# Reading a pair's first bank ahead of the next unit's low part, and adding its sums a unit later

## The chip, the cores and the metric

The kernel runs on one core of a Trainium2 chip. The metric is the time of one execution on the device in microseconds (us), as the median of several runs. TensorE (PE in the rows) multiplies; VectorE (DVE) and ScalarE (ACT) split operands, empty PSUM banks and do the elementwise work; GpSimd (POOL) and SyncE (SP, which issues the loads) help. The engines run on their own and meet at semaphores.

## The reference

Two transformer blocks run one after the other on x, 256 tokens by 2048 channels in float32. The attention, convolution and recurrence parts are not touched by this change. What is touched is where the two MLPs add their last product to x:

```python
def first_block(x, ...):
    ...
        x = x + merged @ w_out[l]
        h = rms_norm(x, norm_mlp_g[l]) @ w_mlp_up[l]             # 2048 -> 8192
        x = x + jnp.square(jax.nn.relu(h)) @ w_mlp_down[l]       # 8192 -> 2048

def second_block(x, ...):
    ...
        x = x + mix @ w_out[l]
        h2 = _rms_norm(x, norm2_g[l])
        x = x + (jax.nn.silu(h2 @ w_gate[l]) * (h2 @ w_up[l])) @ w_down[l]   # 2048 -> 5632 -> 2048
```

## The kernel before

**A product in two parts.** Every float32 operand is split into a high part, rounded to the type that TensorE multiplies fast, and a low part, the rest. A product is high by high, plus low by high, plus high by low. A weight tile of 1 MB (128 rows by 4 blocks of 512) is a *unit*. SyncE loads it into `raw` (four buffers), ScalarE writes its high part `whi` (line 422), VectorE subtracts and writes its low part `wlo` (line 430, `lo_unit`), and TensorE runs first the products with `whi`, then those with `wlo`. `whi` and `wlo` have two buffers each, so ScalarE and VectorE work at most about one unit ahead of TensorE. Semaphores `hi_split`, `lo_split` and `units_used` count these steps.

**A pair.** In the last product of the first MLP (kind `scaled`: six pairs in `PAIRS1`, since the result is multiplied by the squared inverse norm) and in the whole second MLP (17 pairs in `PAIRS`, kinds `gate` and `down`) two blocks of 512 output columns are made at once, for two halves of 128 tokens. The four results stand in four PSUM banks `acc[:, b, m]`, here called bank (b, m). A scaled pair has 8 units, as have a gate pair and the later down pairs; the first two down pairs have 6. In an ordinary unit TensorE runs 24 matmuls, 6 for each bank. In the first and the last unit of a pair it does so bank by bank (`plain_products`): in the first, it waits in `bank_free` before each bank until VectorE has read what the pair before left there; in the last, it raises `bank_done` after each bank, and `units_used` after bank (1, 1).

**Seven units.** Two units of a pair (numbers 3 and 5; in the second MLP's first two down pairs number 3 alone, then 1 and 3) use seven products of sums in the place of eight: 21 matmuls (`seven_products`, `seven_low`). Part of their results lands in other banks, `sd` and `tp`. After the pair's last `lo_unit` VectorE runs `combine`: three instructions that make `vw` and `yz` from `tp`, `sd` and `q_sum` (ScalarE's copy of `sd`, counted by `q_copied`) and raise the semaphore `combined` three times.

**How a pair ends.** VectorE has then seven or eight instructions to do on x (`xres`): four that add the banks (`bank_to_x`, lines 2350 and 2352) and three or four that add `q_sum`, `vw` and `yz` (`sums_to_x`, lines 2364 and 2371 to 2375). For a scaled pair `finish_scaled` holds all of them, in the order bank (0, 0), bank (0, 1), sums, bank (1, 0), bank (1, 1); for a down pair `finish_first` and `finish` give the same order. All of it stands behind the `lo_unit` of the next unit. That next unit is the first of another pair, or, after the second scaled pair of each of three quarters, the first unit of the MLP's up product (`up_products`, line 474), which needs both banks (0, m). A gate pair is not added to x: its first bank is read by `finish_first` *ahead* of the next `lo_unit`, and the others behind it.

**What sets the order.** Each engine's program is written out by hand, one function per engine with plain Python loops; the order of the calls is the order of the instructions. Nothing is scheduled. A boundary between pairs, in what follows, is the last unit of one pair and the first of what comes after. Three boundaries lead from a scaled pair to a scaled pair, three from a scaled pair to an up product, and five out of a down pair (three to the other down pair, two to a gate pair). The last down pair has no successor.

Of the kernel before, what the change touches and what calls it, by code (L numbers as in the profile page):

```python
# [35 lines left out]
MT = T // P  # L36
# [89 lines left out]
def build(nc, t, out):  # L126

    ctx = ExitStack()
    with ctx:
# [409 lines left out]
        PAIRS = []  # L539
# [12 lines left out]
        for p in PAIRS1 + PAIRS:  # L552
            ahead = PAIRS1[:p.n] if p.kind == "scaled" else PAIRS1 + PAIRS[:p.n]
            p.order = len(ahead)
            p.combined = sum(3 if q.kind == "gate" else 6 for q in ahead)
            p.gates = sum(q.kind == "gate" for q in ahead)
            p.sevens = sum(len(q.seven) for q in ahead)
            p.seven_units = [q.unit + v for q in ahead for v in q.seven]
            p.q_sum = q_sums[p.kind != "scaled"]
# [911 lines left out]
        def _(pe):  # L1471
# [271 lines left out]
            def seven_products(p, v, hi, lo):  # L1743
# [11 lines left out]
                if first:  # L1755

                    if p.order:
                        pe.wait_ge(combined, p.combined)
                        pe.wait_ge(q_copied, p.order)
                    if p.kind == "scaled":  # L1760
                        pe.wait_ge(read_dve, read_first(PAIRS1[p.n // 2 * 2]))
                    else:
                        pe.wait_ge(op_lo, T_HID2 + p.turned * MT)
# [159 lines left out]
        def _(dve):  # L1923
# [453 lines left out]

            def finish_scaled(p):

                for m in range(MT):  # L2380
                    bank_to_x(p, 0, m)
                dve.wait_ge(read_dve, read_first(p) + MT)
                sums_to_x(p)
                for m in range(MT):
                    bank_to_x(p, 1, m)

# [30 lines left out]
            for i in range(QUARTERS):  # L2417
                for p in PAIRS1[2 * i:2 * i + 2]:
                    for v in range(p.units):
                        if v in p.seven:  # L2420
                            seven_low(p, v)
                        else:
                            lo_unit(dve, (p.unit + v) // UN, v % UN)
                        if p.chunk[1] == 0 and v == 0:
                            hidden_squares(i * UN + UN - 1, i * 2 * UN + G_DLOOP)
                        if p.chunk[1] == 0 and v == 1:
                            hidden_lo(i * UN + UN - 1, UN - 1)
                        if p.chunk[1] and v == 0:
                            finish_scaled(PAIRS1[p.n - 1])
                        if v == p.units - 1:  # L2430
                            combine(p)
                for c in range(UN):
                    g = i * 2 * UN + G_DLOOP + UN + c
                    for j in range(UN):
                        lo_unit(dve, g, j)
                        if c == 0 and j == 0:
                            finish_scaled(PAIRS1[2 * i + 1])
                        if c and j == 0:
# [166 lines left out]
            def finish(p):  # L2605

                if p.kind == "down":
                    bank_to_x(p, 0, 1)
                    if p is not PAIRS[-1]:
                        dve.wait_ge(bank_read, 4 * p.n + MT)  # L2610
                        sums_to_x(p)
                    for m in range(MT):
# [13 lines left out]
            for p in PAIRS:  # L2626
                for v in range(p.units):
                    if v == 0 and p.n and PAIRS[p.n - 1].kind == "gate":
                        finish_first(PAIRS[p.n - 1])
                    if v in p.seven:  # L2630
                        seven_low(p, v)
                    else:
                        lo_unit(dve, (p.unit + v) // UN, (p.unit + v) % UN)
                    if v == 0 and p.n and PAIRS[p.n - 1].kind == "down":
                        finish_first(PAIRS[p.n - 1])
                    if p.n == 0 and v < UN:
# [35 lines left out]
```

## Time and profile before

| | |
|---|---|
| median of 3 runs | 2473.7 us (2473.68 to 2473.72) |
| the profiled execution: time | 2474.51 us |
| the profiled execution: span of the core | 2472.8 us |
| TensorE busy | 2453.8 us, 99% |
| VectorE busy | 1708.5 us, 69% |
| ScalarE busy | 1212.2 us, 49% |
| chain that ended last | PE 93%, DVE 4%, ACT 1%, issue 1% |
| mean DMA rate | 189 GB/s |

The rows are of one profiled execution. In a timeline each row has the start and the duration in us; `x2` says that two such instructions followed each other, and a bracket says how long the engine had been idle before and what it waited for. `L2350` is line 2350 of the kernel before. A row of a matmul lasts longer than the distance to the next, because matmuls overlap; it is the distance between starts that adds up to time.

### The profile page before, as it was taken

Reading aid. Unit: us, or ns where it says so; the run is one execution under the profiler, and the core shown is the slowest. Engines: PE = TensorE matmul, PEld = TensorE weight load, DVE = VectorE, ACT = ScalarE, POOL = GpSimd, SP = SyncE. Lnnn points to the kernel's source line nnn. Section 1 sums busy time; section 2 is a strip of 40 time slices with the busy share of each in tenths; the row PEclk is TensorE's granted clock in tenths of the full one; section 3 lists DMA queues with packets and bytes.
Section 4 is the critical chain, followed back from the end, with each engine's and each line's share of the span. In section 5 each row is a group of like instructions: output and inputs, shape, how many; then the busy total and the mean of one; then the engine's idle time right before and its main releaser. Section 6 shows DMA issues by size and latency. Waiting matters only on the chain.

```text
span 2472.8 us, 28758 instructions
## 1 busy us (share of the span) xinstructions
PE 2453.8 (99%) x11719; PEld 2047.9 (83%) x11719; DVE 1708.5 (69%) x1590; ACT 1212.2 (49%) x1270; POOL 116.6 (5%) x95
## 2 busy tenths in 40 slices
PE   9999999999999999999999999999999999999999
PEld 8888888888888878888888888788888788878887
DVE  5775455454655785776765558886788878887887
ACT  5545534343344444544444448875555444544553
POOL 0410010010110000000000010000200000000000
PEclk9999999999999999999999999999999999999999
DMA  7555465666655565655665655444556565655654
GB/s 252 173 184 180 160 192 192 196 194 196 230 184 187 187 201 188 197 192 175 201 194 192 209 171 189 153 151 162 180 191 199 190 194 185 207 195 191 203 187 153
DMA packets 233138, 467.18 MB, mean 189 GB/s; under 512 B 13424, under 2 KB 25216, under 8 KB 232622
## 3 DMA queue, kind: packets, MB, share of 16 engines
q1 hardware_dynamic: 231454, 460.09, 57.4%
q10 hardware_dynamic: 1552, 5.25, 0.6%
q8 instruction: 93, 1.52, 0.3%
q14 instruction: 39, 0.32, 0.0%
HBM read 463.20 MB, written 2.10 MB: 188 GB/s over the span
## 4 chain that ended last, share of the span: by engine, by line
PE 93%; DVE 4%; ACT 1%; issue 1%; POOL 0%; DMA 0%; ACTq 0%; DVEq 0%; POOLq 0%
PE acc L445 13%; PE acc L454 13%; PE acc L447 13%; PE acc L1714 9%; PE acc L1715 9%; PE acc L1718 9%; PE acc L474 5%; PE acc L480 2%; PE sd L474 2%; PE tp L474 2%; DVE wlo L430 1%; PE tp L480 1%; PE sd L480 1%; PE acc L1772 1%; PE acc L1768 1%; PE acc L1769 1%
## 5 line engine op out<-in xcount | busy, mean ns | idle before, releaser
L430 DVE TENSOR_TENSOR wlo<-raw,whi 128x2048 fp32r<-128x2048 f32 (+1 forms) x396 | 913.5, 2308 | 642.9 <-ACT whi L422 641.8
L422 ACT ACTIVATE whi<-raw 128x2048 fp32r<-128x2048 f32 (+1 forms) x396 | 748.0, 1890 | 844.4 <-PE acc L454 356.4
L445 PE MATMUL acc<-whi,opA_hi 128*128 128x512 f32 x1152 | 454.8, 395 | 0.0
L447 PE MATMUL acc<-whi,opA_lo 128*128 128x512 f32 x1152 | 449.4, 390 | 0.0
L454 PE MATMUL acc<-wlo,opA_hi 128*128 128x512 f32 x1152 | 287.4, 391 | 0.2 <-DVE wlo L430 0.2
L445 PEld LDWEIGHTS acc<-whi,opA_hi 128*128 128x128 f32 x1152 | 216.9, 188 | 45.4 <-issue 0.9
L447 PEld LDWEIGHTS acc<-whi,opA_lo 128*128 128x128 f32 x1152 | 216.8, 188 | 44.2
L454 PEld LDWEIGHTS acc<-wlo,opA_hi 128*128 128x128 f32 x1152 | 214.9, 188 | 44.8 <-DVE wlo L430 0.8
L1714 PE MATMUL acc<-whi,opA_hi 128*128 128x512 f32 x552 | 216.0, 391 | 5.9 <-DVE xres L2350 3.8
L1715 PE MATMUL acc<-whi,opA_lo 128*128 128x512 f32 x552 | 215.0, 389 | 0.0
L1714 PE MATMUL acc<-whi,opB 128*128 128x512 f32 x536 | 209.7, 391 | 1.4 <-DVE xres L2352 1.4
L1715 PE MATMUL acc<-whi,opB 128*128 128x512 f32 x536 | 208.7, 389 | 0.0
L474 PE MATMUL acc<-opB,whi 128*128 128x512 f32 x512 | 159.2, 392 | 1.1 <-DVE xres L2350 1.1
L445 PE MATMUL acc<-whi,opB 128*128 128x512 f32 (+1 forms) x384 | 147.5, 387 | 2.0 <-ACT whi L422 2.0
L1718 PE MATMUL acc<-wlo,opA_hi 128*128 128x512 f32 x552 | 148.1, 389 | 0.0
L447 PE MATMUL acc<-whi,opB 128*128 128x512 f32 (+1 forms) x384 | 145.1, 381 | 0.0
L1718 PE MATMUL acc<-wlo,opB 128*128 128x512 f32 x536 | 143.1, 389 | 0.0
L1714 PEld LDWEIGHTS acc<-whi,opA_hi 128*128 128x128 f32 x552 | 103.6, 188 | 30.4 <-DVE xres L2350 5.0
L1718 PEld LDWEIGHTS acc<-wlo,opA_hi 128*128 128x128 f32 x552 | 103.6, 188 | 21.7
L1715 PEld LDWEIGHTS acc<-whi,opA_lo 128*128 128x128 f32 x552 | 103.7, 188 | 21.0
L1714 PEld LDWEIGHTS acc<-whi,opB 128*128 128x128 f32 x536 | 100.6, 188 | 23.1 <-DVE xres L2352 2.2
L1718 PEld LDWEIGHTS acc<-wlo,opB 128*128 128x128 f32 x536 | 100.6, 188 | 20.9
(417 smaller groups left out, 3373.9 us busy)
## 6 DMA issues: line engine op xcount, KB each, us to landing
raw<-in_w_in SPq DMA_DIRECT2D x114, 1024.0 KB, 5.4
raw<-in_w_mlp_up SPq DMA_DIRECT2D x64, 1024.0 KB, 5.5
raw<-in_w_mlp_down SPq DMA_DIRECT2D x64, 1024.0 KB, 5.0
raw<-in_w_gate SPq DMA_DIRECT2D x88, 512.0 KB, 3.8
raw<-in_w_up SPq DMA_DIRECT2D x88, 512.0 KB, 4.7
raw<-in_w_down SPq DMA_DIRECT2D x88, 512.0 KB, 4.7
raw<-in_w_out SPq DMA_DIRECT2D x32, 1024.0 KB, 5.0
raw<-in_w_branch SPq DMA_DIRECT2D x16, 1024.0 KB, 5.0
```

Source lines behind the costliest of these rows:

```text
L422: eng.activation(whi[:, j % SPL, k, 0:cols], raw[:, j, k, 0:cols], ACT.Copy).then_inc(hi_split, share(k))
L430: eng.tensor_tensor(wlo[:, j % SPL, k, 0:cols], raw[:, j, k, 0:cols], whi[:, j % SPL, k, 0:cols].bitcast(F32), ALU.subtract).then_inc(lo_s ...
L445: eng.matmul(acc[:, pair, m, 0:cols], hi[:, kt + i, m * P:(m + 1) * P], whi[:, s, i, 0:cols], start=first and i == 0, stop=False)
L447: eng.matmul(acc[:, pair, m, 0:cols], lo[:, kt + i, m * P:(m + 1) * P], whi[:, s, i, 0:cols], start=False, stop=False)
L454: mm = eng.matmul(acc[:, pair, m, 0:cols], hi[:, kt + i, m * P:(m + 1) * P], wlo[:, s, i, 0:cols], start=False, stop=last and i == UK - 1)
L474: eng.matmul(up_bank(group, c), whi[:, s, i, c * P:(c + 1) * P], opB[:, UK * j + i, :, :].rearrange("p v t -> p (v t)"), start=j == 0 and ...
L480: mm = eng.matmul(up_bank(group, c)[:, 0:T], wlo[:, s, i, c * P:(c + 1) * P], opB[:, UK * j + i, 0, :], start=False, stop=j == UN - 1 and ...
L1714: pe.matmul(acc[:, b, m, :], hi[:, 2 * v + a, rows], whi[:, s, 2 * a + b, :], start=first and a == 0, stop=False)
L1715: pe.matmul(acc[:, b, m, :], lo[:, 2 * v + a, rows], whi[:, s, 2 * a + b, :], start=False, stop=False)
L1718: return pe.matmul(acc[:, b, m, :], hi[:, 2 * v + a, m * P:(m + 1) * P], wlo[:, s, 2 * a + b, :], start=False, stop=last and a == 1)
L1768: pe.matmul(bank, a_h, seven_hi[:, i, :], start=alone and first, stop=False)
L1769: pe.matmul(bank, a_l, seven_hi[:, i, :], start=False, stop=False)
```

## The change

The banks and the sums of a scaled or down pair are no longer added in one go behind the next `lo_unit`.

- Ahead of the `lo_unit` of the next pair's first unit VectorE now reads bank (0, 0); ahead of that of an up product, banks (0, 0) and (0, 1). The other banks follow behind that `lo_unit`.
- `sums_to_x` comes a unit later, behind the `lo_unit` (or `seven_low`) of the next unit, with a wait that the bank reads are done.
- TensorE's wait before a pair's first seven unit asks for the three steps of `combine` of the pair before (`p.sums_read`) and no longer for all six.

The numbers of instructions, their shapes and the programs of the other engines are the same but for that wait. The diff:

```diff
--- before.py
+++ after.py
@@ -553,6 +553,8 @@
             ahead = PAIRS1[:p.n] if p.kind == "scaled" else PAIRS1 + PAIRS[:p.n]
             p.order = len(ahead)
             p.combined = sum(3 if q.kind == "gate" else 6 for q in ahead)
+
+            p.sums_read = ahead[-1].combined + 3 if ahead else 0
             p.gates = sum(q.kind == "gate" for q in ahead)
             p.sevens = sum(len(q.seven) for q in ahead)
             p.seven_units = [q.unit + v for q in ahead for v in q.seven]
@@ -1755,7 +1757,7 @@
                 if first:
 
                     if p.order:
-                        pe.wait_ge(combined, p.combined)
+                        pe.wait_ge(combined, p.sums_read)
                         pe.wait_ge(q_copied, p.order)
                     if p.kind == "scaled":
                         pe.wait_ge(read_dve, read_first(PAIRS1[p.n // 2 * 2]))
@@ -2375,14 +2377,11 @@
                 dve.tensor_tensor(xres[:, :, n2], xres[:, :, n2], yz[:, :, :], ALU.add).then_inc(combined, 1)
                 dve.wait_ge(combined, p.combined + 6)
 
-            def finish_scaled(p):
-
-                for m in range(MT):
-                    bank_to_x(p, 0, m)
-                dve.wait_ge(read_dve, read_first(p) + MT)
-                sums_to_x(p)
-                for m in range(MT):
-                    bank_to_x(p, 1, m)
+            def banks_to_x(p, ahead):
+
+                for b, m in ((0, 0), (0, 1), (1, 0), (1, 1)):
+                    if ahead(b, m):
+                        bank_to_x(p, b, m)
 
             for n in range(UN):
                 for j in range(UN):
@@ -2417,6 +2416,8 @@
             for i in range(QUARTERS):
                 for p in PAIRS1[2 * i:2 * i + 2]:
                     for v in range(p.units):
+                        if p.chunk[1] and v == 0:
+                            banks_to_x(PAIRS1[p.n - 1], lambda b, m: (b, m) == (0, 0))
                         if v in p.seven:
                             seven_low(p, v)
                         else:
@@ -2426,15 +2427,23 @@
                         if p.chunk[1] == 0 and v == 1:
                             hidden_lo(i * UN + UN - 1, UN - 1)
                         if p.chunk[1] and v == 0:
-                            finish_scaled(PAIRS1[p.n - 1])
+                            banks_to_x(PAIRS1[p.n - 1], lambda b, m: (b, m) != (0, 0))
+                        if p.chunk[1] and v == 1:
+                            dve.wait_ge(read_dve, read_first(p))
+                            sums_to_x(PAIRS1[p.n - 1])
                         if v == p.units - 1:
                             combine(p)
                 for c in range(UN):
                     g = i * 2 * UN + G_DLOOP + UN + c
                     for j in range(UN):
+                        if c == 0 and j == 0:
+                            banks_to_x(PAIRS1[2 * i + 1], lambda b, m: b == 0)
                         lo_unit(dve, g, j)
                         if c == 0 and j == 0:
-                            finish_scaled(PAIRS1[2 * i + 1])
+                            banks_to_x(PAIRS1[2 * i + 1], lambda b, m: b == 1)
+                        if c == 0 and j == 1:
+                            dve.wait_ge(read_dve, read_first(PAIRS1[2 * i + 1]) + 2 * MT)
+                            sums_to_x(PAIRS1[2 * i + 1])
                         if c and j == 0:
                             hidden_squares((i + 1) * UN + c - 1, g)
                         if c and j == 1:
@@ -2606,9 +2615,6 @@
 
                 if p.kind == "down":
                     bank_to_x(p, 0, 1)
-                    if p is not PAIRS[-1]:
-                        dve.wait_ge(bank_read, 4 * p.n + MT)
-                        sums_to_x(p)
                     for m in range(MT):
                         bank_to_x(p, 1, m)
                     return
@@ -2625,14 +2631,15 @@
 
             for p in PAIRS:
                 for v in range(p.units):
-                    if v == 0 and p.n and PAIRS[p.n - 1].kind == "gate":
+                    if v == 0 and p.n:
                         finish_first(PAIRS[p.n - 1])
                     if v in p.seven:
                         seven_low(p, v)
                     else:
                         lo_unit(dve, (p.unit + v) // UN, (p.unit + v) % UN)
-                    if v == 0 and p.n and PAIRS[p.n - 1].kind == "down":
-                        finish_first(PAIRS[p.n - 1])
+                    if v == 1 and p.n and PAIRS[p.n - 1].kind == "down":
+                        dve.wait_ge(bank_read, 4 * p.n)
+                        sums_to_x(PAIRS[p.n - 1])
                     if p.n == 0 and v < UN:
                         side2(12 * UN + v)
                     if v == 0 and p.n:
```

The order of VectorE's instructions at three places follows. In the rows, `wlo<-raw,whi` is a `lo_unit`, `xres<-acc` a bank read, `xres<-` with `q_sum`, `vw` or `yz` a sum, and `t_sum` and `seven_lo` belong to `seven_low`. Lines 2338, 2350 and 2364 of before are lines 2340, 2352 and 2366 after.

VectorE, from `combine` of the first scaled pair of a quarter to the second pair's second unit, before:

```order
L2338 TENSOR_TENSOR yz<-vw,sd 128x1024
L430 TENSOR_TENSOR wlo<-raw,whi 128x2048
L2350 SCALAR_TENSOR_TENSOR xres<-acc,smalls,xres 128x512 x2
L2364 SCALAR_TENSOR_TENSOR xres<-q_sum,smalls,xres 128x512
L2364 SCALAR_TENSOR_TENSOR xres<-vw,rstd_neg,xres 128x512
L2364 SCALAR_TENSOR_TENSOR xres<-yz,smalls,xres 128x512 x2
L2350 SCALAR_TENSOR_TENSOR xres<-acc,smalls,xres 128x512 x2
L430 TENSOR_TENSOR wlo<-raw,whi 128x2048 x2
```

The same place of VectorE in the changed kernel:

```order
L2340 TENSOR_TENSOR yz<-vw,sd 128x1024
L2352 SCALAR_TENSOR_TENSOR xres<-acc,smalls,xres 128x512
L430 TENSOR_TENSOR wlo<-raw,whi 128x2048
L2352 SCALAR_TENSOR_TENSOR xres<-acc,smalls,xres 128x512 x3
L430 TENSOR_TENSOR wlo<-raw,whi 128x2048
L2366 SCALAR_TENSOR_TENSOR xres<-q_sum,smalls,xres 128x512
L2366 SCALAR_TENSOR_TENSOR xres<-vw,rstd_neg,xres 128x512
L2366 SCALAR_TENSOR_TENSOR xres<-yz,smalls,xres 128x512 x2
L430 TENSOR_TENSOR wlo<-raw,whi 128x2048
```

One bank read moved ahead of the low part, and the four sums moved behind the next low part. The boundaries out of a down pair, but for the one below, read the same with the lines of the down kind.

VectorE, from `combine` of a quarter's second scaled pair into the up product, in the changed kernel (before, it read as the first fence):

```order
L2340 TENSOR_TENSOR yz<-vw,sd 128x1024
L2352 SCALAR_TENSOR_TENSOR xres<-acc,smalls,xres 128x512 x2
L430 TENSOR_TENSOR wlo<-raw,whi 128x2048
L2352 SCALAR_TENSOR_TENSOR xres<-acc,smalls,xres 128x512 x2
L430 TENSOR_TENSOR wlo<-raw,whi 128x2048
L2366 SCALAR_TENSOR_TENSOR xres<-q_sum,smalls,xres 128x512
```

Here two bank reads stand ahead of the low part.

VectorE, from the first down pair of the second MLP into the second, whose unit 1 is a seven unit, before:

```order
L430 TENSOR_TENSOR wlo<-raw,whi 128x2048
L2352 TENSOR_TENSOR xres<-acc,xres 128x512 x2
L2371 TENSOR_TENSOR xres<-xres,q_sum_149 128x512
L2373 TENSOR_TENSOR xres<-xres,vw 128x512
L2375 TENSOR_TENSOR xres<-xres,yz 128x2x512
L2352 TENSOR_TENSOR xres<-acc,xres 128x512 x2
L2272 TENSOR_TENSOR t_sum<-raw 128x1024
```

The same place in the changed kernel:

```order
L430 TENSOR_TENSOR wlo<-raw,whi 128x2048
L2354 TENSOR_TENSOR xres<-acc,xres 128x512 x3
L2274 TENSOR_TENSOR t_sum<-raw 128x1024
L2277 TENSOR_TENSOR t_sum<-t_sum,raw 128x512
L2279 TENSOR_TENSOR t_sum<-t_sum,raw 128x512
L2283 TENSOR_TENSOR seven_lo<-raw,seven_hi 128x512
L2284 TENSOR_TENSOR seven_lo<-raw,seven_hi 128x1024
L2288 TENSOR_TENSOR seven_lo<-t_sum,seven_hi 128x2048
L2373 TENSOR_TENSOR xres<-xres,q_sum_149 128x512
L2375 TENSOR_TENSOR xres<-xres,vw 128x512
L2377 TENSOR_TENSOR xres<-xres,yz 128x2x512
L430 TENSOR_TENSOR wlo<-raw,whi 128x2048
```

Here the sums stand between unit 1, a seven unit, and the low part of unit 2.

## Rows read from the trace of the kernel before

**Rows 1.** The page: span, TensorE's busy time and share, and its granted clock.

```profile
span 2472.8 us, 28758 instructions
...
PE 2453.8 (99%) x11719; PEld 2047.9 (83%) x11719; DVE 1708.5 (69%) x1590; ACT 1212.2 (49%) x1270; POOL 116.6 (5%) x95
...
PEclk9999999999999999999999999999999999999999
```

**Rows 2.** TensorE's waits: total us, times, longest us.

```profile
PE acc L1714 <- DVE xres L2350: 3.8, 3, 1.3
PE acc L1714 <- DVE xres L2352: 3.5, 5, 0.7
...
PE acc L474 <- DVE xres L2350: 1.1, 3, 0.4
...
PE sd L1772 <- DVE seven_lo L2282: 0.5, 1, 0.5
```

**Rows 3.** Timeline of TensorE, first unit after a scaled pair: start, duration.

```profile
878.13 0.44 PE L1714 MATMUL acc<-whi,opA_hi 128*128 128x512 f32 x1
...
882.35 0.50 PE L1714 MATMUL acc<-whi,opA_hi 128*128 128x512 f32 x1 [1.27 <-DVE xres L2350]
...
885.20 0.39 PE L1714 MATMUL acc<-whi,opA_hi 128*128 128x512 f32 x1
```

**Rows 4.** Timeline of VectorE at the same boundary.

```profile
873.20 1.22 DVE L2338 TENSOR_TENSOR yz<-vw,sd 128x1024 f32<-128x1024 f32 x1
874.99 2.29 DVE L430 TENSOR_TENSOR wlo<-raw,whi 128x2048 fp32r<-128x2048 f32 x1 [0.57 <-ACT whi L422]
877.20 1.40 DVE L2350 SCALAR_TENSOR_TENSOR xres<-acc,smalls,xres 128x512 f32<-128x512 f32 x2
...
881.54 1.41 DVE L2350 SCALAR_TENSOR_TENSOR xres<-acc,smalls,xres 128x512 f32<-128x512 f32 x2
...
887.78 2.29 DVE L430 TENSOR_TENSOR wlo<-raw,whi 128x2048 fp32r<-128x2048 f32 x1 [2.63 <-ACT whi L422]
```

**Rows 5.** Timelines at a boundary from gate pair to gate pair: VectorE, TensorE.

```profile
1991.03 0.69 DVE L2603 TENSOR_TENSOR acc<-acc,q_sum 128x512 f32<-128x512 f32 x1
...
1994.82 0.39 PE L1714 MATMUL acc<-whi,opB 128*128 128x512 f32 x1
...
2000.27 1.03 PE L500 MATMUL tp<-ident,stage 128*128 128x128 f32 x8
```

**Rows 6.** Timeline of TensorE, last scaled matmuls and first up units.

```profile
921.47 0.61 PE L1718 MATMUL acc<-wlo,opA_hi 128*128 128x512 f32 x2
922.45 0.73 PE L474 MATMUL acc<-opB,whi 128*128 128x512 f32 x2 [0.37 <-DVE xres L2350]
...
928.13 0.63 PE L474 MATMUL acc<-opB,whi 128*128 128x512 f32 x2
...
933.70 0.63 PE L474 MATMUL acc<-opB,whi 128*128 128x512 f32 x2
```

**Rows 7.** Timeline of TensorE, first unit after the second down pair.

```profile
1951.61 0.39 PE L1714 MATMUL acc<-whi,opB 128*128 128x512 f32 x1
...
1958.10 0.39 PE L1714 MATMUL acc<-whi,opB 128*128 128x512 f32 x1
```

**Rows 8.** Timeline of TensorE, second down pair: starts of units 0 and 2.

```profile
1918.47 0.40 PE L1714 MATMUL acc<-whi,opA_hi 128*128 128x512 f32 x1
...
1930.53 0.39 PE L1714 MATMUL acc<-whi,opA_hi 128*128 128x512 f32 x1
```

**Rows 9.** Timeline of VectorE over the same units.

```profile
1918.86 0.69 DVE L2371 TENSOR_TENSOR xres<-xres,q_sum 128x512 f32<-128x512 f32 x1
...
1921.32 1.29 DVE L2352 TENSOR_TENSOR xres<-acc,xres 128x512 f32<-128x512 f32 x2
1922.53 1.22 DVE L2272 TENSOR_TENSOR t_sum<-raw 128x1024 f32<-128x1024 f32 x1
...
1926.85 2.29 DVE L2286 TENSOR_TENSOR seven_lo<-t_sum,seven_hi 128x2048 fp32r<-128x2048 f32 x1
```

## The prediction

> **What bounds the kernel now.** First the page's totals: TensorE is busy for 2453.8 of 2472.8 us, 99%, at the full granted clock in every slice [rows 1]. Only its idle time, some 19 us, and what stands around it can be won without taking products away. So the second view is TensorE's waits. Four of them are at ends of pairs: 3.8 us in 3 waits for a scaled bank read (line 2350), 3.5 us in 5 for a down bank read (line 2352), 1.1 us in 3 ahead of the up product, and 0.5 us once for the low part of a seven unit [rows 2]. Together 8.9 us. The third view is the timelines of TensorE and VectorE at one such place.
>
> At the first one, TensorE starts the new pair's bank (0, 0) at 878.13, has to start bank (1, 0) at 882.35 after 1.27 us of idleness, and comes to the second unit at 885.20 [rows 3]. VectorE meanwhile ends `combine` at 873.20 + 1.22 = 874.42, waits 0.57 us for ScalarE's high part, makes the low part from 874.99, reads two banks from 877.20, does the four sums, and reads the other two banks from 881.54 [rows 4]. The bank that TensorE waits for is late by the sums. They take 881.54 - 877.20 less two reads (1.40) = 2.9 us.
>
> **What a stall costs.** I take distances between starts and not the bracketed idleness. A clean first unit is the one after a gate pair: 2000.27 - 1994.82 = 5.45 us for 24 matmuls, 0.227 us each [rows 5]. Against it:
> - Scaled to scaled: 885.20 - 878.13 = 7.07 [rows 3], excess 1.62. Three times, by the waits view of nearly one size (3.8 us, longest 1.3) [rows 2]: 4.9 us.
> - Scaled to up: the last two scaled matmuls start at 921.47, so the up product could start at 921.47 + 2 x 0.227 = 921.92. It starts at 922.45, and its first unit takes 928.13 - 922.45 = 5.68, where the next takes 933.70 - 928.13 = 5.57 [rows 6]. Excess 0.53 + 0.11 = 0.64, three times: 1.9 us.
> - Out of a down pair: 1958.10 - 1951.61 = 6.49 [rows 7], excess 1.04. Four of the five: 4.2 us.
> - The fifth, into the pair whose unit 1 is a seven unit: units 0 and 1 take 1930.53 - 1918.47 = 12.06 [rows 8], clean 5.45 + 21 x 0.227 = 10.22. Excess 1.8 us, both waits of that pair in it.
>
> Sum: 4.9 + 1.9 + 4.2 + 1.8 = 12.8 us.
>
> The excess of 1.62 is more than the 1.27 us in the bracket, since the first matmuls after a wait are also further apart than 0.227. By the brackets alone the sum would be 8.9 us. The Trainium skill ("Perfetto Trace Analysis", section "Tensor Engine Instruction (MATMUL, LD_WEIGHTS)") says that the reported end of a matmul is estimated from its size and not observed. By that page idleness, which is counted from such an end, is not to be summed, and distances of starts are, which gives the 12.8; the trace agrees, as the rows above differ by those 0.35 us.
>
> **The change, part by part.**
>
> *Bank (0, 0) ahead of the low part.* It costs one read, 0.7 us (half of 1.40 [rows 4]), in front of an instruction that TensorE needs. The read can begin when `combine` is done, at 874.42, and its bank is done too: TensorE's last unit starts at 878.13 - 5.45 = 872.68 and is through with bank (0, 0) after a quarter, at 874.04, plus the tail of a matmul and the signal, together some 0.3 us. VectorE then stood idle for 0.57 us until 874.99 [rows 4], so the read ends at about 875.1 and the low part starts 0.1 to 0.2 us later than before. It ends at 877.4. TensorE needs it behind the first four matmuls of the new pair, at 878.13 + 0.91 = 879.04. Margin 1.6 us: the read costs nothing. The nearest row that shows such a read is the one after a gate pair: VectorE does it ahead of the low part at 1991.03, and that unit is the clean one [rows 5]. There it stands at eleven boundaries. From this row I take the cost as zero; the upper bound is 0.2 us at each of eleven places, 2.2 us, if nothing hid it.
>
> *The other banks right behind.* (0, 1) is read by 878.0, (1, 0) by 878.7, and (1, 1), whose products end only with the unit at 878.13, by about 879.4. TensorE needs them at 879.5, 880.9 and 882.2, a quarter of a unit apart. Margins 1.5, 2.2 and 2.8 us, so no stall remains at the plain boundaries. A down bank read is a plain add and no longer than that.
>
> *Two banks ahead of the up product.* Bank (0, 1) is done half a unit into TensorE's last unit, at 921.92 - 2.72 = 919.2 plus 0.3. Its read ends at 920.2, and TensorE wants it at 921.92. The low part then runs to about 922.5; TensorE wants it behind 16 matmuls, at 925.55. It comes 1.4 us later than before, and with it the release of its `raw` buffer and a load that SyncE has queued behind that. That buffer's next user is four units away, so I charge nothing.
>
> *The sums a unit later.* The same 2.9 us now stand behind the low part of unit 1. Ahead of unit 2's low part VectorE was idle for 2.63 us, waiting for ScalarE [rows 4], and the sums and a read have left unit 0, which brings unit 1's low part forward by up to 2.5 us (it then waits for its own high part). So low part 2 can start as soon as its high part is there; it is needed 3.6 us into unit 2, and the margin is over 4 us. What waits for the sums, `q_copied` and `combine` of the new pair, is four units away. The loads don't wait for them.
>
> *The tightest place.* In the second down pair unit 1 is a seven unit. Its `t_sum` starts at 1922.53 less the sums (1921.32 - 1918.86 = 2.46) less one read (0.6) = 1919.5 [rows 9]. The last `seven_lo` starts 1926.85 - 1922.53 = 4.32 later, at 1923.8, when the part that TensorE waited 0.5 us for is just done; TensorE wants that at 1918.47 + 5.45 + 1.36 = 1925.3. That wait goes too. Then come 2.3 us, the sums (2.46) and unit 2's low part (2.2), to 1930.7, and unit 3, again a seven unit, has its first low parts at 1930.7 + 4.3 = 1935.0. TensorE, now ahead by 1.8 us, wants them at 1918.47 + 5.45 + 4.77 + 5.45 + 1.36 = 1935.5. Margin 0.5 us; if it fails, a few tenths, once.
>
> *The wait on* `combined`. At unit 1 of that pair TensorE would otherwise wait for sums that stand behind the low parts it needs. With the weaker wait it asks for `combine`, done a unit before. Cost zero.
>
> So the sum stays 12.8 us, with bounds 12.8 and 12.8 - 2.2 - 0.3 = 10.3; it cannot be above the excess measured, since nothing else on TensorE is taken away. The profiled execution takes 2474.5 us, 0.8 above the median: it should come to 2461.7, its span to 2460.0, and the median to 2473.7 - 12.8 = **2460.9 us**. The last down pair and its stores are unchanged.
>
> **The rivals.**
>
> *Only the bracketed idleness comes back.* If the wider spacing after a wait belonged to the start of a pair, 8.9 us would go: 2464.8. Against it: a gate boundary has no such spacing [rows 5]. 10%.
>
> *The first bank is reported late (the other side).* VectorE runs in order, and now waits at `bank_done` ahead of the low part. If that signal came only with the last unit's end, the read would run from 878.3 to 879.0 and the low part to 881.3, 2.3 us after TensorE wants it: 8 x 2.3. The up products would get their two banks about 1.6 us after the unit's end: 3 x 1.6. That is 23.2 us new against 12.8 gone: 2473.7 + 10.4 = 2484.1. It begins to cost from a delay of 1.6 us, the low part's margin, and makes the kernel slower from about 2.8 us. Against it: the read after a gate pair at 1991.03, which waits for the same signal, starts 1.7 us and not a whole unit into TensorE's last unit (which began at 1994.82 - 5.45 = 1989.37) [rows 5]. 5%, and another 3% for a part of it that leaves the time where it was. The Trainium skill (same page, same section) lets a matmul push its semaphore update once PSUM has acknowledged its bytes; by that the delay is a tail of the single matmul, and this rival is void; the row at 1991.03 agrees.
>
> *The change doesn't free TensorE.* If its waits before banks (0, 1) and (1, 0) counted reads in another order than VectorE now makes them, the stalls would stay: 2473.7. Both go (0, 0), (0, 1), (1, 0), (1, 1), so 4%.
>
> **How the numbers follow.** Forecast 2460.9 with 78%, its own bounds 2460 to 2463.4. Only the idleness: 10%. Late signal: 5% slower, 3% no change; no effect: 4%. The range reaches from 2459.5, for stalls that were a little larger than the rows, to 2465.0, which takes in the second case. A measurement of this kernel can tell about 0.2%, 4.9 us, from no change. Faster by more: 0.78 + 0.10 = 0.88; within: 0.07; slower: 0.05.
>
> **What would show it.** In TensorE's waits the rows for lines 2350 and 2352 (now 2352 and 2354) and for `seven_lo` are gone; the first unit of every pair takes 5.45 us, and the up product starts 0.227 us after the last scaled matmul. VectorE's read of bank (0, 0) starts right behind `combine`, at the latest 2 us into TensorE's last unit. Wrong it would be if TensorE waited for `wlo` (line 430) in a first unit, if units 2 or 3 of a pair took longer, or if the spans of the boundaries shrank and others grew.

## The result, and the profile after

| | before | after |
|---|---|---|
| median | 2473.68 us | 2460.62 us |
| the profiled execution: time | 2474.51 us | 2460.66 us |
| its span | 2472.8 us | 2458.9 us |
| TensorE busy | 2453.8 us | 2448.9 us |
| chain that ended last, PE share | 93% | 97% |

The changed kernel is faster by 13.1 us, ratio 0.9947 with a 95% interval of 0.9932 to 0.9962. The forecast was 2460.9 us. The medians are of five executions each; one of the five of the changed kernel took 5014.87 us, twice the others, for a reason that nothing on record shows, and the ratio leaves it out.

The page of the changed kernel, its totals, the granted clock and the shares of the chain that ended last (answers to [rows 1]):

```profile
span 2458.9 us, 28747 instructions
...
PE 2448.9 (100%) x11719; PEld 2048.8 (83%) x11719; DVE 1707.2 (69%) x1590; ACT 1212.4 (49%) x1270; POOL 116.6 (5%) x95
...
PEclk9999999999999999999999999999999999999999
...
PE 97%; DVE 1%; ACT 1%; issue 0%; POOL 0%; DMA 0%; ACTq 0%; DVEq 0%; POOLq 0%
```

TensorE's waits in the changed kernel, all of them (total us, times, longest us):

```profile
PE acc L445 <- ACT whi L422: 2.0, 3, 1.1
PE sd L1633 <- POOL ones L832: 1.2, 1, 1.2
PE tp L1825 <- ACT q2T L1305: 0.8, 1, 0.8
PE sd L1650 <- DMA gain_rows<-in_norm_mix_g: 0.7, 1, 0.7
PE tp L500 <- POOL stage L911: 0.7, 1, 0.7
PE tp L500 <- DVE opA_lo L512: 0.4, 1, 0.4
PE acc L454 <- DVE wlo L430: 0.2, 1, 0.2
```

All four rows of [rows 2] are gone: no wait for a bank read, none ahead of the up product, none for the low part of the seven unit. The others were there before and are elsewhere in the kernel. The 11 instructions that the page has fewer are semaphore instructions of VectorE (741, not 752); the computing instructions are the same in number.

The first boundary between scaled pairs, timeline of VectorE in the changed kernel:

```profile
872.21 1.22 DVE L2340 TENSOR_TENSOR yz<-vw,sd 128x1024 f32<-128x1024 f32 x1
873.35 0.74 DVE L2352 SCALAR_TENSOR_TENSOR xres<-acc,smalls,xres 128x512 f32<-128x512 f32 x1
874.01 2.28 DVE L430 TENSOR_TENSOR wlo<-raw,whi 128x2048 fp32r<-128x2048 f32 x1
876.21 2.06 DVE L2352 SCALAR_TENSOR_TENSOR xres<-acc,smalls,xres 128x512 f32<-128x512 f32 x3
879.44 2.29 DVE L430 TENSOR_TENSOR wlo<-raw,whi 128x2048 fp32r<-128x2048 f32 x1 [1.17 <-ACT whi L422]
...
885.18 2.29 DVE L430 TENSOR_TENSOR wlo<-raw,whi 128x2048 fp32r<-128x2048 f32 x1 [0.68 <-ACT whi L422]
```

TensorE at the same place: the last unit, the new pair's first and second unit.

```profile
871.69 0.39 PE L1716 MATMUL acc<-whi,opA_hi 128*128 128x512 f32 x1
...
877.13 0.39 PE L1716 MATMUL acc<-whi,opA_hi 128*128 128x512 f32 x1
...
882.57 0.39 PE L1716 MATMUL acc<-whi,opA_hi 128*128 128x512 f32 x1
```

The first unit takes 882.57 - 877.13 = 5.44 us where [rows 3] showed 7.07. VectorE reads the first bank in what was its 0.57 us of idleness in [rows 4]; the low part follows without a gap, 2.32 us after the start of TensorE's last unit as before (2.31), and the sums, between the two later low parts, still leave 0.68 us ahead of unit 2.

Before the up product the changed TensorE shows this, last scaled matmuls and first two up units:

```profile
918.84 0.61 PE L1720 MATMUL acc<-wlo,opA_hi 128*128 128x512 f32 x2
919.29 0.62 PE L474 MATMUL acc<-opB,whi 128*128 128x512 f32 x2
...
924.83 0.63 PE L474 MATMUL acc<-opB,whi 128*128 128x512 f32 x2
```

The step is 0.45 us, two matmuls; in [rows 6] it was 0.98. VectorE there reads the second bank and then makes the low part:

```profile
916.78 0.75 DVE L2352 SCALAR_TENSOR_TENSOR xres<-acc,smalls,xres 128x512 f32<-128x512 f32 x1 [0.53 <-PE acc L1720]
917.44 2.28 DVE L430 TENSOR_TENSOR wlo<-raw,whi 128x2048 fp32r<-128x2048 f32 x1
```

**What the profile has besides.** The span fell by 13.9 us, the median by 13.1. The first place that the change touches lies at 870 us, and TensorE was already 1.0 us ahead there. The difference is in the first microseconds. The first row of eight low-part matmuls (line 454) after 40 us of the span starts at 41.60 before and at 40.63 after; over all runs below this mark lies between 40.24 and 43.48. So spans compare only from this mark on. Before, 2472.8 - 41.60 = 2431.2; after, 2458.9 - 40.63 = 2418.3, which is 12.9 us less. TensorE's busy time fell too, by 4.9 us, though it runs the same 11719 matmuls: the wider spacing, after a wait and in the first microseconds, counts as busy in the page, and the brackets miss it.

### The profile page after: what moved, and what is told of

Read it like the earlier page. It is cut to its first block, busy times and chain, and to the rows that moved or that the text cites. A ratio compares the mean times of both kernels' runs of the same rounds, so it can differ in the third digit from the quotient of the medians.

```text
span 2458.9 us, 28747 instructions
## 1 busy us (share of the span) xinstructions
PE 2448.9 (100%) x11719; PEld 2048.8 (83%) x11719; DVE 1707.2 (69%) x1590; ACT 1212.4 (49%) x1270; POOL 116.6 (5%) x95
## 4 chain that ended last, share of the span: by engine, by line
PE 97%; DVE 1%; ACT 1%; issue 0%; POOL 0%; DMA 0%; ACTq 0%; DVEq 0%; POOLq 0%
PE acc L454 13%; PE acc L445 13%; PE acc L447 13%; PE acc L1716 10%; PE acc L1717 10%; PE acc L1720 10%; PE acc L474 5%; PE acc L480 2%; PE tp L474 2%; PE sd L474 2%; PE sd L480 1%; PE tp L480 1%; PE acc L1774 1%; PE acc L1771 1%; PE acc L1770 1%; PE tp L500 1%
```

## The experiments

All were built from the changed kernel unless said otherwise. "From the mark" is the span less the start of that row, which takes the start-up out; it is of one profiled execution of each run, and the two of the changed kernel (the one above and e5) agree within 0.1 us. e5 is the changed kernel once more, on one chip with e6 to e8.

> The changed kernel itself, beside the next three on one chip. 2460.6 us, 13.1 us under the kernel before; the mark for the three others.

It took 2460.90 us, ratio 0.9947 (0.9932 to 0.9962).

| run | median us | span | mark | from the mark | against e5 |
|---|---|---|---|---|---|
| before (the profiled execution) | 2473.8 (beside e5) | 2472.8 | 41.60 | 2431.2 | +12.8 |
| e1 scaled only | 2466.63 | 2465.3 | 41.03 | 2424.3 | +5.9 |
| e2 down only | 2467.88 | 2466.5 | 41.30 | 2425.2 | +6.8 |
| e3 sums later only | 2463.78 | 2462.5 | 41.48 | 2421.0 | +2.7 |
| e4 bank ahead only | 2466.74 | 2465.8 | 41.60 | 2424.2 | +5.8 |
| e5 the changed kernel | 2460.90 | 2458.6 | 40.24 | 2418.4 | 0 |
| e6 two banks ahead | 2461.16 | 2458.9 | 40.26 | 2418.6 | +0.3 |
| e7 three banks ahead | 2469.10 | 2468.4 | 41.72 | 2426.7 | +8.3 |
| e8 strong wait | 2467.87 | 2468.6 | 43.48 | 2425.1 | +6.8 |
| e9 thin sums, after | 2460.85 | 2458.2 | 40.44 | 2417.8 | -0.6 |
| e10 thin sums, before | 2462.84 | 2460.3 | 40.24 | 2420.1 | +1.7 |
| e11 up ahead, sums later | 2461.50 | 2460.2 | 41.23 | 2419.0 | +0.6 |

### Each half alone (e1, e2)

e1 puts the down pairs back, e2 the scaled pairs.

```diff
--- e1
                     bank_to_x(p, 0, 1)
+                    if p is not PAIRS[-1]:
+                        dve.wait_ge(bank_read, 4 * p.n + MT)
+                        sums_to_x(p)
...
-                    if v == 0 and p.n:
+                    if v == 0 and p.n and PAIRS[p.n - 1].kind == "gate":
                         finish_first(PAIRS[p.n - 1])
...
-                    if v == 1 and p.n and PAIRS[p.n - 1].kind == "down":
-                        dve.wait_ge(bank_read, 4 * p.n)
-                        sums_to_x(PAIRS[p.n - 1])
+                    if v == 0 and p.n and PAIRS[p.n - 1].kind == "down":
+                        finish_first(PAIRS[p.n - 1])
```

> Only the scaled pairs have the change; the second MLP's down pairs end as before. By my sum (distances between starts) 4.9 + 1.9 = 6.8 us go: 2473.7 - 6.8 = 2466.9 us. By the bracketed idleness alone 3.8 + 1.1 = 4.9 us go: 2468.8 us. In TensorE's waits the rows for the scaled bank reads are gone and the one for the down bank reads (3.5 us, 5 times) stays.

> Only the down pairs have the change; the scaled pairs end as before. By my sum 4.2 + 1.8 = 6.0 us go: 2467.7 us. By the bracketed idleness 3.5 + 0.5 = 4.0 us go: 2469.7 us. The waits for scaled bank reads stay (3.8 and 1.1 us), those for down bank reads and for the low part of the seven unit are gone. If the two halves are independent, their gains add up to that of the whole change, 13.1 us.

e1 took 2466.63 us, ratio 0.9971 (0.996 to 0.9982); e2 2467.88, ratio 0.9976 (0.9967 to 0.9985). From the mark e1 is 6.9 us under before and e2 6.0, together 12.9, the whole change; by the medians, against the kernel before beside them (2473.96), it is 7.3 and 6.1. My sums were 6.8 and 6.0, those of the brackets 4.9 and 4.0. Of the rows of [rows 2] each keeps the other half's, and only those. TensorE's waits of e1:

```profile
PE acc L1716 <- DVE xres L2354: 3.5, 5, 0.7
...
PE sd L1774 <- DVE seven_lo L2284: 0.5, 1, 0.5
```

So the halves are independent, and a stall costs what the starts say, not what its bracket says.

### Which of the two moves does it (e3, e4, e11)

e3 leaves all bank reads behind the low part and moves only the sums. e4 reads ahead and leaves the sums in place. e11 is e3 with the two banks ahead of the up product.

```diff
--- e3 (e11 has these hunks, but not the two of the up product)
-                        if p.chunk[1] and v == 0:
-                            banks_to_x(PAIRS1[p.n - 1], lambda b, m: (b, m) == (0, 0))
...
-                            banks_to_x(PAIRS1[p.n - 1], lambda b, m: (b, m) != (0, 0))
+                            banks_to_x(PAIRS1[p.n - 1], lambda b, m: True)
...
-                        if c == 0 and j == 0:
-                            banks_to_x(PAIRS1[2 * i + 1], lambda b, m: b == 0)
...
-                            banks_to_x(PAIRS1[2 * i + 1], lambda b, m: b == 1)
+                            banks_to_x(PAIRS1[2 * i + 1], lambda b, m: True)
--- e4
                         if p.chunk[1] and v == 0:
-                            banks_to_x(PAIRS1[p.n - 1], lambda b, m: (b, m) != (0, 0))
-                        if p.chunk[1] and v == 1:
-                            dve.wait_ge(read_dve, read_first(p))
+                            bank_to_x(PAIRS1[p.n - 1], 0, 1)
+                            dve.wait_ge(read_dve, read_first(PAIRS1[p.n - 1]) + MT)
                             sums_to_x(PAIRS1[p.n - 1])
+                            banks_to_x(PAIRS1[p.n - 1], lambda b, m: b == 1)
```

The down pairs and, in e4, the up product have the same.

> All four bank reads stand behind the next low part as before, and only the sums come a unit later. Theory: the sums were what made bank (1, 0) late, and bank (0, 0) was in time anyway (read at 877.95, wanted at 878.13), so almost everything at the eight plain boundaries goes; left are the up products' 3 x 0.64 = 1.9 us and some 0.07 us at each of eight boundaries: 2460.6 + 2.4 = 2463.0 us. Rival: the first bank's read ahead of the low part is what frees TensorE; then most of the 13 us stay and the time is near 2472.

> The first bank (both first banks before an up product) is read ahead of the low part, and the sums stay where they were, between banks (0, 1) and (1, 0). Theory: bank (1, 0) of a scaled pair is read at 8.85 us after the start of TensorE's last unit and wanted at 8.16, so 0.7 us of idleness (0.85 with the slower first matmuls) stays three times; of a down pair at 8.4, so 0.4 us stays four times, and about 1.3 us in the pair whose unit 1 is a seven unit; nothing before the up products. Left 2.6 + 1.6 + 1.3 = 5.5 us: 2460.6 + 5.5 = 2466.1 us. Rival (the read ahead does it all): 2460.6 us.

> The sums a unit later, and both first banks ahead of the low part before an up product, but at the eight plain boundaries no bank is read ahead. Theory: bank (0, 0) is read 0.1 to 0.2 us before TensorE wants it, and only the spacing of its first matmuls suffers, 0.06 to 0.1 us at each of eight boundaries: 0.5 to 0.8 us above the changed kernel, 2461.4 to 2461.7 us. If the read ahead at the plain boundaries is worth nothing at all: 2460.9 us.

e3: 2463.78 us, ratio 0.9958 (0.9942 to 0.9975). The sums a unit later are four fifths of the gain: 10.2 of 12.8 us from the mark. The expectation had 2.4 us left; from the mark it is 2.7, and the 0.3 us between them are lost in unit 3 of the second down pair (below, at e11). Most of what is left is the wait before the up product, unchanged, 0.7 us each time from start to start:

```profile
PE acc L474 <- DVE xres L2352: 1.1, 3, 0.4
```

e4: 2466.74 us, ratio 0.9972 (0.9962 to 0.9983), 5.8 us above the changed kernel where 5.5 were expected. TensorE's waits of e4, then its bank (1, 0) after a scaled pair, and the same after the second down pair:

```profile
PE acc L1716 <- DVE xres L2352: 2.0, 3, 0.7
...
PE sd L1774 <- DVE seven_lo L2284: 0.5, 1, 0.5
```

```profile
880.37 0.61 PE L1720 MATMUL acc<-wlo,opA_hi 128*128 128x512 f32 x2
881.66 0.50 PE L1716 MATMUL acc<-whi,opA_hi 128*128 128x512 f32 x1 [0.68 <-DVE xres L2352]
...
1949.32 0.61 PE L1720 MATMUL acc<-wlo,opB 128*128 128x512 f32 x2
1950.05 0.50 PE L1716 MATMUL acc<-whi,opB 128*128 128x512 f32 x1
```

After the scaled pair 0.68 us are in a bracket. After the down pair TensorE starts 0.73 us behind the two matmuls that take 0.45, so it waited 0.28 us, and no bracket and no row of the waits says so. The row of the two matmuls is 0.61 us long and ends at 1949.93, so that most of this short wait lies inside it.

e11: 2461.50 us, ratio 0.9949 (0.9933 to 0.9966), 0.6 us above the changed kernel both by the medians and from the mark, in the range expected. So the read ahead at the eight plain boundaries is worth 0.6 us in all. But it is not spread over the eight as the expectation had it. Set beside the changed kernel's, matmul by matmul, TensorE of e11 loses 0.1 us at each of the three scaled boundaries, at most 0.03 us at each down boundary, and 0.3 us at one place more: unit 3 of the second down pair, the tightest place of the prediction. There the read that stands behind the low part makes the whole chain of low parts later, and the first product with a low part starts 0.40 us after the one before it, not 0.227 (e3 loses the same 0.3 us):

```profile
1928.27 0.39 PE L1771 MATMUL acc<-seven_hi,ad_lo 128*128 128x512 f32 x1
1928.67 0.50 PE L1774 MATMUL sd<-seven_lo,opA_hi 128*128 128x512 f32 x1
```

The range was met, but half of the loss came from a place that the expectation did not name. At the first scaled boundary of e11 TensorE's first row of the new pair lasts 0.43 us, not 0.39:

```profile
877.76 0.43 PE L1716 MATMUL acc<-whi,opA_hi 128*128 128x512 f32 x1
```

That agrees with the bank being ready only just in time, as in [rows 3], where the same row lasts 0.44. Before the up product the read ahead is worth 2.1 us (e3 against e11), 0.7 for each of three.

### The length of the sums (e9, e10)

Both add only one column in 512 of `q_sum`, `vw` and `yz`; e9 from the changed kernel, e10 from the kernel before.

```diff
-                        ins = dve.scalar_tensor_tensor(xres[:, m, n], src, by[:, m:m + 1], xres[:, m, n], ALU.mult, ALU.add)
+                        c1 = slice(n.start, n.start + 1)
+                        ins = dve.scalar_tensor_tensor(xres[:, m, c1], src[:, 0:1], by[:, m:m + 1], xres[:, m, c1], ALU.mult, ALU.add)
...
```

The three additions of the down kind are cut to one column in the same way.

> The changed kernel, with its sums cut to one column of 512 (the rest of q_sum, vw and yz is never added to x, so the output isn't the reference's). VectorE saves some 2.3 us at each of eleven boundaries. Theory: where the change puts the sums they cost nothing, so nothing is won: 2460.9 us as the changed kernel on this chip, at most 0.3 us less from the last pair's end. Rival (the sums still delay low parts a unit later, in a way the waits don't show): over 1 us less.

> The kernel before, with its sums cut to one column in the same way (the output isn't the reference's). Everything stands in the old order. Theory: the length of the sums was the whole cause of the stalls at the eight plain boundaries, so bank (1, 0) is in time and they vanish; the three up products still wait for bank (0, 1), which is read ahead of the sums: 3 x 0.64 us. As with the sums a unit later: 2463.3 to 2463.8 us. Rival (the order of the first read matters there too): above 2466 us.

e9: 2460.85 us against 2460.90, and 0.6 us less from the mark. The traces say where the 0.6 us are: in the end of the last pair, whose sums and bank reads have no TensorE work behind them. TensorE's last matmuls of the changed kernel (first line) and of e9 (second):

```profile
2454.61 0.61 PE L1720 MATMUL acc<-wlo,opA_hi 128*128 128x512 f32 x2
...
2454.43 0.61 PE L1720 MATMUL acc<-wlo,opA_hi 128*128 128x512 f32 x2
```

From the mark to this row it is 2454.61 - 40.63 = 2413.98 us and 2454.43 - 40.44 = 2413.99; from the row to the end 4.3 and 3.8. So where the change puts them the sums cost TensorE nothing, and the thin ones save 0.5 us at the end, not the 0.3 at most that I had given. The medians, 0.05 us apart, don't show it, since the start-up scatters by more.

e10: 2462.84 us, ratio 0.9955 (0.994 to 0.997), half a microsecond below the range that I gave. That half is the same end: from e10's last matmuls, at 2456.49, it is 3.8 us too. Of the 11.1 us that it gains from the mark 10.6 are stalls that go with no instruction moved. Only the row before the up product stays in its waits (1.1 us, 3 times). Up to the last matmuls e10 is 0.5 us better than e3, and 0.3 of them are the tightest place, where e10 loses nothing. So two ways of taking the sums out from between the banks, later or shorter, agree within 0.5 us.

### How much margin the low part has (e6, e7)

```diff
--- e6 (e7 has 3 where this has 2)
-                            banks_to_x(PAIRS1[p.n - 1], lambda b, m: (b, m) == (0, 0))
+                            banks_to_x(PAIRS1[p.n - 1], lambda b, m: 2 * b + m < 2)
...
-                            banks_to_x(PAIRS1[p.n - 1], lambda b, m: (b, m) != (0, 0))
+                            banks_to_x(PAIRS1[p.n - 1], lambda b, m: 2 * b + m >= 2)
...
-                    bank_to_x(p, 0, 0)
+                    for k in range(2 if p is not PAIRS[-1] else 1):
+                        bank_to_x(p, k // 2, k % 2)
...
```

> At the plain boundaries banks (0, 0) and (0, 1) are read ahead of the low part, as before an up product. T is the start of TensorE's last unit. Bank (0, 1) is reported at T + 2.93 (in the changed kernel's trace the read before an up product starts 2.93 us after T), so the low part runs from T + 3.6 to T + 5.9 and is wanted at T + 5.44 + 0.91 = 6.35: margin 0.45 us. Theory: no cost at seven boundaries; at the eighth, whose unit 1 is a seven unit, the chain to unit 3 has a margin of 0.48 us and comes 0.8 us later, so 0.3 us are lost once: 2460.9 us. If a bank were reported only at the end of the unit, the low part would end at T + 9.1 or later and 2.8 us be lost at each of eight boundaries: 2483 us.

> Banks (0, 0), (0, 1) and (1, 0) are read ahead of the low part at the plain boundaries. Bank (1, 0) is reported at T + 4.29, the low part runs from T + 4.95 to T + 7.25 and is wanted at T + 6.35. Theory: TensorE waits 0.9 us for the low part, 1.1 us with the slower matmuls behind the wait, at each of eight boundaries, and 0.2 us more once: 2460.6 + 9.0 = 2469.6 us, still faster than before. In TensorE's waits a row for line 454's kind of low part in the pairs (wlo, line 430) appears eight times. Rival (the low part has more slack than I think): 2460.6 us.

e6: 2461.16 us, 0.3 above e5 as expected. The loss is where it was placed, and set beside the changed kernel's matmuls nowhere else. TensorE of e6 in unit 3 of the second down pair, last product with the high part and first with the low one:

```profile
1927.01 0.39 PE L1771 MATMUL acc<-seven_hi,ad_lo 128*128 128x512 f32 x1
1927.43 0.50 PE L1774 MATMUL sd<-seven_lo,opA_hi 128*128 128x512 f32 x1
```

The step is 0.42 and not 0.227. The changed kernel shows the 0.48 us of margin that e6 used up: there VectorE's part ends at 1925.89 + 1.22 = 1927.11 and TensorE takes it at 1927.59.

```profile
1925.89 1.22 DVE L2284 TENSOR_TENSOR seven_lo<-raw,seven_hi 128x1024 fp32r<-128x1024 f32 x1
...
1927.59 0.39 PE L1774 MATMUL sd<-seven_lo,opA_hi 128*128 128x512 f32 x1
```

e7: 2469.10 us, ratio 0.998 (0.9971 to 0.999), 8.2 us above e5 (9.0 expected). From start to start it loses 1.0 to 1.1 us at each of the eight boundaries; of the 0.2 us more that the expectation had for unit 3 only 0.05 is there. Its waits and VectorE at the first boundary:

```profile
PE acc L1720 <- DVE wlo L430: 5.9, 8, 0.8
```

```profile
874.47 0.74 DVE L2352 SCALAR_TENSOR_TENSOR xres<-acc,smalls,xres 128x512 f32<-128x512 f32 x1
875.74 0.75 DVE L2352 SCALAR_TENSOR_TENSOR xres<-acc,smalls,xres 128x512 f32<-128x512 f32 x1 [0.52 <-PE acc L1720]
877.10 0.75 DVE L2352 SCALAR_TENSOR_TENSOR xres<-acc,smalls,xres 128x512 f32<-128x512 f32 x1 [0.61 <-PE acc L1720]
877.77 2.28 DVE L430 TENSOR_TENSOR wlo<-raw,whi 128x2048 fp32r<-128x2048 f32 x1
```

The reads follow each other by the quarter of a unit that a bank takes, 877.10 - 875.74 = 1.36 us. Each bank is reported by itself, which settles the rival of a late signal, and TensorE's new wait is for the low part, eight times, 0.8 us at most. The order "banks first" is thus free for one, nearly free for two, and costs most of the gain for three.

### The wait on `combined` (e8)

```diff
-                        pe.wait_ge(combined, p.sums_read)
+                        pe.wait_ge(combined, p.combined)
```

> TensorE's wait ahead of a pair's first seven unit asks again for all six steps of the pair before, the sums too. Theory: at one place only, the pair whose first seven unit is unit 1, the sums stand behind that unit's low parts: they end at 1920.40 in the changed kernel's trace, and TensorE could start the unit at 1916.03. It loses 4.4 us once, 2465.0 us; elsewhere the first seven unit is unit 3 and the sums are long done. Rival (the weaker wait matters nowhere): 2460.6 us.

e8: 2467.87 us, ratio 0.9976 (0.9967 to 0.9986), 7.0 us above e5, where 4.4 were expected. The place is the expected one, and the only one. TensorE of e8 at unit 1 of the second down pair and at unit 2:

```profile
1918.41 0.61 PE L1720 MATMUL acc<-wlo,opA_hi 128*128 128x512 f32 x2
1923.29 0.79 PE L1770 MATMUL sd<-seven_hi,opA_hi 128*128 128x512 f32 x1 [4.27 <-DVE xres L2377]
1923.88 0.63 PE L1771 MATMUL sd<-seven_hi,opA_lo 128*128 128x512 f32 x1
1924.31 0.63 PE L1770 MATMUL acc<-seven_hi,opA_hi 128*128 128x512 f32 x1
...
1927.72 0.63 PE L1771 MATMUL sd<-seven_hi,ad_lo 128*128 128x512 f32 x1
1928.15 0.46 PE L1770 MATMUL tp<-seven_hi,ad_hi 128*128 128x512 f32 x1
...
1930.50 0.39 PE L1716 MATMUL acc<-whi,opA_hi 128*128 128x512 f32 x1
```

The unit starts 1923.29 - 1918.86 = 4.4 us late. It then takes 1930.50 - 1923.29 = 7.2 us where 21 x 0.227 = 4.8 are normal: eleven matmuls stand 0.43 to 0.6 us apart. The windows view of e8 shows the granted clock (columns: stretch, length, busy us of PE, PEld, DVE, ACT, POOL with counts, PE clock, DMA share, GB/s):

```profile
1915.00:1920.00 5.00, 4.02 (x18) 3.00 (x16) 4.93 (x6) 2.98 (x3) 0.00 (x0) 1.00 0.41 151
1920.00:1925.00 5.00, 1.71 (x4) 1.42 (x5) 4.91 (x5) 1.05 (x1) 0.00 (x0) 0.64 0.53 182
1925.00:1930.00 5.00, 5.00 (x16) 3.94 (x16) 3.14 (x4) 0.00 (x0) 0.00 (x0) 0.67 0.70 234
1930.00:1935.00 5.00, 5.00 (x23) 4.14 (x23) 2.55 (x3) 3.48 (x4) 0.00 (x0) 1.00 0.01 3
```

During the idle 4.3 us the clock fell from its full level (2.4 GHz) to half (1.2 GHz); the means of 0.64 and 0.67 are mixtures of the two. The record of the clock in the trace has the half level from 1921.45 to 1928.27. So the wait costs 4.4 us of idleness and 2.4 us of half speed. The Trainium skill ("TensorE: Matmul & The Clock Gate", "Part 1: The HAM clock gate") says that the clock is halved after idleness and given back after sustained activity; the trace agrees. None of the stalls of the kernel before, 1.3 us at most, had this effect: its record is at the full level without a break from 10.49 to 2471.5 us of the span. The page alone would not tell, since its row of 40 slices reads 9 throughout for e8 as well.

## Why the prediction was right, step by step

- *Cause.* The sums stood between banks (0, 1) and (1, 0), and bank (1, 0) came late. Shown from two sides: moving them away (e3) and shortening them (e10) removes the stalls at all eight plain boundaries; what is left there is 0.1 us or less each, and in e3 0.3 us once.
- *Size of a stall from starts.* 4.9 + 1.9 = 6.8 and 4.2 + 1.8 = 6.0 against 6.9 and 6.0 from the mark. The prediction measured one place of each kind and multiplied. Matmul by matmul the traces of before and after differ by 1.63 to 1.65 us at the three scaled boundaries (1.62 predicted), 0.66 to 0.67 before the up products (0.64), 1.01 to 1.05 at four down boundaries (1.04) and 1.85 at the fifth (1.8), so the places of a kind were alike. The rival by the brackets (2464.8 us for the whole) is refuted, and e4's rows after a down pair show why: a wait of 0.28 us without any bracket.
- *The first bank ahead costs nothing.* Its read ended at T + 2.4 us, T being the start of TensorE's last unit, as worked out; the low part started no later than before, where 0.1 to 0.2 us were allowed, and no wait for a low part appeared. e7 shows the wait that comes when the margin is overdrawn. The prediction did not say how little this read gives at the plain boundaries: 0.6 of 12.8 us, half of it at the tightest place. It is needed before the up products, where it gives 2.1 us.
- *Two banks ahead of the up product.* Bank (0, 1) was expected at 3.0 us after T and read 2.93 us after it; TensorE goes from one product to the other in 0.45 us.
- *The sums a unit later are hidden.* VectorE still waits 0.68 us for the high part ahead of unit 2; e9 wins nothing on TensorE by shortening them, and half a microsecond at the kernel's end.
- *The tightest place.* Margin 0.5 us worked out, 0.48 in the trace. e6, e11 and e3 each overdraw it a little and lose 0.3 us there.
- *The wait on* `combined`. "Cost zero" was right for the weaker wait; that the change needs it was said, but not for how much. It is 7 us, over half of the gain, and my expectation of e8 put it at 4.4, since it left out the clock.
- *The profiled execution.* A time of 2461.7 us and a span of 2460.0 were forecast; 2460.66 and 2458.9 came. The 1.0 to 1.1 us between them are the start-up, which the prediction did not treat; from the mark the gain is 12.9 us where 12.8 were worked out.
- *The rivals.* A late signal: refuted by the reads of e7, and by the first read of the changed kernel, which starts at T + 1.66 us. No effect: refuted by the waits and the time.

## What to carry to other kernels

Where a consumer empties several buffers that a producer refills in turn, put only the emptying between them, and do everything else that the same results need later. Sum a stall by the distance between starts, against a clean place of the same shape; brackets left out 30% of it here, and a wait of 0.28 us wholly. When work moves past the point where another engine's wait counts it, move the wait's number too: the strong wait alone would have given back 7 of 13 us.

## What the runs showed of the hardware

- After 4.3 us without a matmul TensorE came back at half clock for eleven matmuls, 2.4 us lost beyond the wait (e8). Stalls of up to 1.3 us left the clock full and cost only some 0.35 us more than their bracket.
- The start of the kernel scatters by up to 3 us between executions (marks from 40.24 to 43.48 us). Part of it is in the first product: in the trace before, its first six steps are 0.42 to 0.58 us long and then 0.23; in the trace after only the first step is long, 0.46 us. The windows view prints a granted clock of 1.00 for both from the start, but the trace's record of the clock begins only at 10.49 us of the span before and at 8.24 after, with the full level, and the view prints 1.00 where there is no record. The steps become short at 10.50 and 8.39, just behind these points, and the long ones, 0.42 to 0.43 us, are the steps of e8 at the half level. So the first matmuls ran at half clock, and how long they did differs between executions: over all runs the record begins between 7.01 (e10) and 13.40 us (e8), and in each trace the steps become short where it begins. In e8 there is also a wait of 0.9 us for the first load of x.
